# Last expert pass: the second half of the gate and up weights as two chunks of two k, for all four experts, each multiplied as it lands

## The reference, cut to what matters

```python
hid = jax.nn.silu(jnp.einsum("nd,edf->nef", x, w_g)) * jnp.einsum("nd,edf->nef", x, w_u)
y = jnp.einsum("nef,efd->nd", hid * gates[:, :, None].astype(x.dtype), w_d)
```

## Time and profile before

| | |
|---|---|
| time, median of 3 runs | 798.68 us (795.09 to 799.47) |
| the profiled execution | 797.72 us |
| its span in the profile | 795.9 us |
| TensorE busy (PE) | 733.8 us, 92% of the span |
| VectorE, ScalarE busy | 312.6 us, 164.3 us |
| moved by DMA | 291.49 MB, mean 366 GB/s |
| mean granted TensorE clock | 0.977 of full |

### The profile page before, as it was taken

How to read it: one execution, slowest core, us unless ns; L and a number is a source line. 1 busy time by engine, 2 the same in 40 slices (tenths; PEclk the granted TensorE clock), 3 DMA queues, 4 the chain that set the end, 5 groups by cost and what they waited for, 6 DMA issues and landing times.

```text
span 795.9 us, 15774 instructions
## 1 busy us (share of the span) xinstructions
PE 733.8 (92%) x6816; PEld 486.3 (61%) x6816; DVE 312.6 (39%) x682; ACT 164.3 (21%) x323; POOL 18.0 (2%) x29
## 2 busy tenths in 40 slices
PE   3999999998899999999976899999999999995987
PEld 2788567677789645655543454689865555553435
DVE  1145668582423733333440231224553334433024
ACT  3113231232211411111110032041241111111004
POOL 0000001011210000000000000001000000000000
PEclk9999999999999999999997999999999999998899
DMA  9999979587799899999999999999789999999992
GB/s 340 386 372 380 356 249 349 182 296 247 214 387 416 335 422 420 410 420 422 420 421 416 402 373 385 387 403 415 284 315 424 412 410 422 420 421 421 412 391 91
DMA packets 92824, 291.49 MB, mean 366 GB/s; under 512 B 11897, under 2 KB 19151, under 8 KB 75343
## 3 DMA queue, kind: packets, MB, share of 16 engines
q1 hardware_dynamic: 81616, 283.79, 91.3%
q10 hardware_dynamic: 11135, 6.64, 2.8%
HBM read 288.32 MB, written 2.10 MB: 365 GB/s over the span
## 4 chain that ended last, share of the span: by engine, by line
PE 73%; SPq 13%; DMA 5%; DVE 3%; ACT 3%; issue 2%; ACTq 0%; DVEq 0%
PE psum L932 7%; PE psum L1435 7%; SPq L769 7%; PE psum L1450 7%; PE psum L1425 6%; PE psum L1351 5%; PE psum L1491 5%; PE psum L1011 5%; PE psum L881 5%; PE psum L1636 4%; PE psum L1654 3%; PE psum L1502 3%; SPq L788 3%; PE psum L1076 2%; DMA ring<-in_w_exp_up 2%
## 5 line engine op out<-in xcount | busy, mean ns | idle before, releaser
L1435 PE MATMUL psum<-ring,hT 128*32 128x512 f32 (+1 forms) x304 | 75.1, 617 | 11.5 <-DMA scratch<-in_w_exp_up 11.5
L1435 PE MATMUL psum<-scratch,hT 128*32 128x512 f32 (+1 forms) x368 | 75.1, 627 | 11.3 <-DMA ring<-in_w_exp_up 11.3
L1425 PE MATMUL psum<-scratch 128*128 128x128 f32 x640 | 75.5, 276 | 0.0
L1425 PEld LDWEIGHTS psum<-scratch 128*128 128x128 f32 x640 | 73.2, 192 | 1.7 <-issue 1.7
L932 PE MATMUL psum<-hT,ring 128*128 128x256 f32 x256 | 57.8, 382 | 1.1 <-DVE hT L2210 0.6
L932 PEld LDWEIGHTS psum<-hT,ring 128*128 128x128 f32 x256 | 47.8, 190 | 9.6 <-DVE hT L2210 2.0
L1502 PEld LDWEIGHTS psum<-const,scratch 128*128 128x128 bf16 x432 | 40.5, 97 | 17.9 <-issue 12.9
L1502 PE MATMUL psum<-const,scratch 128*128 128x256 bf16 x432 | 50.4, 272 | 0.0
L2018 ACT ACTIVATE scratch<-psum 128x256 f32<-128x256 f32 x20 | 7.7, 384 | 199.1 <-PE psum L1435 123.7
L2662 DVE TENSOR_SCALAR hT<-psum,const 128x512 f32<-128x512 f32 x18 | 13.5, 751 | 84.2 <-PE psum L1491 84.2
L1435 PEld LDWEIGHTS psum<-scratch,hT 128*32 128x32 f32 (+1 forms) x368 | 20.5, 118 | 41.9 <-issue 41.9
(11 more groups left out here) (358 smaller groups left out, 989.5 us busy)
## 6 DMA issues: line engine op xcount, KB each, us to landing
ring<-in_w_mod SPq DMA_DIRECT2D x40, 1024.0 KB, 11.5
scratch<-in_w_exp_down SPq DMA_DIRECT2D x32, 1024.0 KB, 18.6
ring<-in_w_exp_down SPq DMA_DIRECT2D x24, 1024.0 KB, 18.2
scratch<-in_w_exp_gate SPq DMA_DIRECT2D x22, 1024.0 KB, 17.2
scratch<-in_w_exp_up SPq DMA_DIRECT2D x22, 1024.0 KB, 19.2
ring<-in_w_exp_gate SPq DMA_DIRECT2D x18, 1024.0 KB, 17.5
ring<-in_w_exp_up SPq DMA_DIRECT2D x18, 1024.0 KB, 19.8
scratch<-in_w_exp_gate SPq DMA_DIRECT2D x24, 512.0 KB, 9.5
```

The lines of the kernel that those rows point to most:

```text
L1425: last = mm(bank[b][:, k * P:(k + 1) * P], hrow[:, t, half * 4 + k, :], Pm[:, t, :], start=(t == 0), stop=(t == 1))
L1435: last = mm(bank[0][i * m:(i + 1) * m, :], xg[:, k, i * m:(i + 1) * m], w[e][:, k, :, :], start=(k == 0), stop=(k == KT - 1))
```

## The change

In the last pass of each layer chunk `c+2` now holds k 4 and 5 of all four experts and chunk `c+3` k 6 and 7 of all four. Each is loaded by the new `quarter_up` as eight transfers of 256 KB with rows of 2 KB. TensorE's new `last_up` waits for `c+2` alone, multiplies its 8 products, gives its slot free, waits for `c+3`, multiplies the other 8 and gives that slot free. Bytes, products and slots are the same. The counts of the semaphores follow (128 for a chunk of eight transfers).

```diff
-        quarters, singles = set(), set()
+        quarters, eighths, singles = set(), set(), set()
...
             quarters.update((moe_at[l] + MOE_SLOTS - 2, moe_at[l] + MOE_SLOTS - 1))
+            eighths.update((moe_at[l] + MOE_SLOTS - 4, moe_at[l] + MOE_SLOTS - 3))
...
-            count[slot_of(c)] += 64 if c in quarters else 16 if c in singles else 32
+            count[slot_of(c)] += 128 if c in eighths else 64 if c in quarters else 16 if c in singles else 32
...
                         for kh in range(2):
+                            if q == NPASS - 1 and kh == 1:
+                                for kq in (2, 3):
+                                    quarter_up(l, c, ids, kq)
+                                    c += 1
+                                continue
...
+            def quarter_up(l, c, ids, kq):
+
+                slot_free(c)
+                s = slot_of(c)
+                for n, e in enumerate(ids):
+                    for a, name in enumerate(("w_exp_gate", "w_exp_up")):
+                        at = (2 * n + a) * 512
+                        w = I[name][l].rearrange("e (p k) f -> e p (k f)", k=KT)
+                        sp.dma_start(slot(s)[:, at:at + 512], w[e][:, 512 * kq:512 * kq + 512]).then_inc(full[s], 16)
...
+            def last_up(n_pass, c):
+
+                pe.wait_ge(S.m_xg1, n_pass + 1)
+                for kq in (2, 3):
+                    slot_full(pe, c + kq)
+                    w = slot(slot_of(c + kq)).rearrange("p (e a k f) -> p e k a f", e=4, a=2, k=2)
+                    for k in range(2):
+                        for i in range(4):
+                            last = mm(bank[0][i * TILE:(i + 1) * TILE, :], xg[:, 2 * kq + k, i * TILE:(i + 1) * TILE],
+                                      w[:, i, k, :, :], start=False, stop=(kq == 3 and k == 1))
+                    used(last)
...
                 for kh in range(2):
+                    if kh == 1 and between is not None:
+                        last_up(n_pass, c)
+                        continue
```

## The result

The changed kernel takes 800.39 us (median of 20 runs, 798.21 to 805.86), the kernel before 798.14 us (20 runs, 795.05 to 800.18). The ratio is 1.0038, with a 95% interval from 1.0025 to 1.005. I had forecast 798.5 us against 798.68, no change that can be measured, with a very small gain; the sign is wrong, and the size came out at that of rival (b), 800.1, though not by its mechanism.

The account below looks back on a forecast made before the run. The prediction took the weight stream to bound the last pass, with TensorE trailing. From the profiled 797.72 us, minus 0.74 (layer 1) plus 0.55 (layer 0) gave 797.5, or 798.5 us on the median's footing, range 796.0 to 800.8.

Parts of the forecast that it names:

- rival (b): TensorE's clock falls after a 2.0 us rest before layer 0's line 1636, costing 1.6 us: 800.1 us; chance 0.23.
- The bound: In the last pass the weight stream leads and TensorE trails; at line 1636 two limits end within 0.2 us.
- TensorE's own work: Last up products: half run early in idle time, the rest take 1.87 us, clock stays up; up ends 3.5 us earlier.
- The transfers: Late up weights in 2 KB rows at 386 GB/s instead of 410: everything behind lands 0.6 us later.
- My upper bound: Slip of the late up landings at most 1.5 us, from a stretch of mixed 2 and 1 KB rows at 357 GB/s.
- my own sign: Wrong in kind if down pieces do not wait, or if landings slip by far more than 1 us.
- Layer 0's sum: Line 1636 waits for later `w_in_odd` weights, landing at 477.8 + 0.6: loss 0.55 us, passed on in full.
- Layer 1's sum: Gain 0.74 us at the down products; 2.8 of the 3.5 us go into waiting for down weights.
- (a): Smaller rows cost nothing; layer 1 gains 1.3 us, layer 0 nothing: 797.3 us; chance 0.14.
- (c): The up phase sets the end and both layers give their 3.5 us: 791.7 us; chance 0.03.
- (d): Fixed price per transfer that the queue does not overlap, 4.6 us a layer: about 806.5 us; chance 0.02.
- The Trainium skill: Its packet cost, 134 cycles for 2 KB rows against 131, put the landings' slip at about 0.2 us.

Follow-up runs that it names:

- e2: The change in layer 1 alone, layer 0 as in the kernel before; ratio to the kernel before 1.0005.
- e3: Kernel before with its chunks and products, but each late up transfer cut in two with rows of 2 KB; ratio to the kernel before 1.0035.
- e4: The changed kernel run again without alteration, for a second profile; ratio to the kernel before 1.004.
- e11: The kernel before run again without alteration, for a second profile; one run, no ratio given.
- e1: The change in layer 0 alone, layer 1 as in the kernel before; ratio to the kernel before 1.004.
- e5: Changed kernel, but SP issues both quarters of each expert's row one right behind the other; ratio to the kernel before 1.0018.
- e10: Changed kernel, but each quarter chunk loads its four gate pieces, then its four up pieces; ratio to the kernel before 1.0027.
- e8: The change in layer 1 alone, with idle products added between the quarters, before the down products and before layer 0's line 1636; ratio to the kernel before 1.0004.
- e9: Changed kernel, but each layer's late quarters are read at the other layer's four expert numbers, from its own tables; ratio to the kernel before 1.0029.

## Why the prediction was wrong, point by point

**The bound** was read rightly. The stream leads in the last pass, TensorE trails it, and line 1636 sits where two limits meet: in the changed kernel `w_in_odd` alone releases it, in both profiles.

**TensorE's own work.** The quarters took 1.93 and 2.50 us in layer 0 and 1.92 each in layer 1; I had 1.87. The first ran without a wait, as said. "I expect the clock to stay up" held between the quarters of layer 1 and nowhere else. In layer 0, and in the down products of both layers, it was at half for all or part of the time (5.33 and 4.48 us for what took 2.79). In layer 0 that was hidden, since line 1667 waited another 1.35 us for its weights. In layer 1 it is most of the missing gain: 36.14 and 36.59 us with the clock down, 35.4 in e2 where it stayed up.

**The transfers: the step that failed.** "I take 0.6, since 386 is measured on the same rows of 2 KB": the slip of the last quarter was 0.52 us in layer 1 and 2.1 and 2.0 in layer 0. The stretch I took 386 from has rows of 2 KB too, but of other tables (`in_w_mod` and `in_w_in_even`), with other places read side by side. e3's S shows that the size of the rows costs about what I said. What I did not price is the order: for each quarter all eight tables are read at the same quarter of a row, and with the four experts of layer 0 those reads run at 355 GB/s. My upper bound, 1.5 us from a stretch at 357 GB/s, was for smaller rows and was still too low: the last up landing was already 2.1 us late, and the loss went on behind the quarters. By my own sign, landings that slip by far more than 1 us, I was wrong in kind in layer 0.

**It went on.** After the last up landing the slip at `w_in_odd` grew from 2.1 to 3.3 us (W). The down transfers are the same, yet the third piece of layer 0 landed at 462.2 + 8.8 = 471.0, 4.4 us after the second (458.3 + 8.3 = 466.6), where before the two were 2.9 apart. One issue on SP was held for 3.2 us (2.3 before), and the DMA share fell to 0.92 between 464 and 467 us at 289 GB/s (1.06 and 383 before). That fits a picture in which some of the 16 engines are behind after the slow reads, SP can't issue past them and the others run dry. The profile doesn't show single engines, so this is argued and not shown.

**Layer 0's sum.** I had a loss of 0.55 us by "477.8 + 0.6"; with the measured slip at that place it is 3.3 (2.8 in e4). The mechanism was right and the term was too small by a factor of five or six. That the loss is passed on in full is borne out by the stretch from this product to layer 1's first up half, which doesn't shrink: 281.55 and 282.11 us in the two profiles before, 281.87 and 282.76 in those of the change.

**Layer 1's sum.** I had 0.74 us gained. Beside 36.36 it is 0.96 in e2's profile, 0.2 in that of the changed kernel and a loss of 0.2 in e4's; beside e11's 36.20 it is 0.8, 0.1 and a loss of 0.4.

**The rivals.** (a), (c) and (d) fell: the smaller rows cost, TensorE waited 1.15 us for the first down piece in layer 1 (in layer 0 no down piece was waited for), and e3, with eight more transfers a layer, slipped by 0.55 and 0.81 us and not by 4.6. (b) met the measured time by chance. Its event shows in e1 and in e2, not in the two profiles of the change. Its condition, the length of the rest, fails too: before line 1636's product rests of 1.91 (e2) and 2.15 us (e1) were followed by the fall, rests of 2.06 (e5) and 2.73 us (e10) were not. e8 shows the other side, a fall behind no long rest.

**The Trainium skill** (DMA: Bandwidth & Descriptors, Why small descriptors are slow) gave some 0.2 us of slip by its cost of a packet, an estimate, and e3 measures 0.55 and 0.81. The 2.0 us a transfer of rival (d) stand in that page's section Anatomy of one DMA, not in Measured, and are a fit for transfers issued by GpSimd, while these are SP's.

## What to carry to other kernels

A rate read from one stretch holds for its pattern of reads, not for its row size alone: before a stream is cut another way, time the new order by itself with the real places, here chosen by the data. When a chunk is cut so that part of it can be used early, ask what everything behind it in the same queue is waiting for; by the prediction's sum 2.8 of the 3.5 us won on TensorE in layer 1 had nowhere to go, and in layer 0 a load two stages later paid. To see one layer's share in a noisy time, compare spans between two events of the same profile.

## What the runs showed of the hardware that I had not expected

The same transfers, of the same size, in the same order, ran at 355 GB/s with the DMA share at 1.03 (changed kernel, layer 0) or at 388 GB/s (layer 1, and e9's layer 0), by which four experts' tables of 1 MB were read. Reading both 2 KB quarters of a row in turn instead of one quarter of all tables first brought the slow case to 386 (e5). Which of the four places make it slow, and why, was not tried.

TensorE's clock fell to 1.2 GHz in e8 right behind seven idle products that filled 1.94 us, with no rest over 0.33 us in the 13 us before. Products of zeros with 32 rows in bf16 did not keep it up there. In e2, with rests of 0.57 and 1.22 us at the same places, it stayed at 2.4 GHz, and in the changed kernel, with rests of 0.58 and 1.15, it fell. The rests in the trace don't tell the two apart.
